# Key pass of a decoder step: value taps loaded later, a gate product moved, one-column factors in scalar form

## The reference

```python
def compress_rows(rows, w1, b1, w2):
    ...
    for j in range(CMP_PARTS):
        h = h + jnp.einsum('bnsgd,sdh->bngh', units[:, j:j + n_cmp], w1p[j])
    return jax.nn.gelu(h) @ w2
...
o_cmp, p_grp = cmp_branch(q, pos, kv['k_cmp'], kv['v_cmp'])
idx, ok = select_blocks(p_grp, pos, kv['n_slc'])
o_slc = kv['slc_fn'](q, pos, idx, ok)
o_win = kv['win_fn'](q, pos)
o = gates[:, :, 0] * o_cmp + gates[:, :, 1] * o_slc + gates[:, :, 2] * o_win
```

## Time and profile before

| what | value |
|---|---|
| median of 3 executions | 3237.72 us (3237.55 to 3238.18) |
| the profiled execution | 3232.46 us |
| its span, first to last instruction | 3230.3 us |
| mean granted clock of TensorE | 0.995 |
| PE busy | 3178.1 us, 98% |
| DVE busy | 1996.0 us, 62% |
| ACT busy | 1553.2 us, 48% |
| POOL busy | 519.0 us, 16% |
| mean DMA rate over the span | 188 GB/s |

### The profile page before, as it was taken

How to read it: one execution, slowest core, us unless ns; L and a number is a source line. 1 busy time by engine, 2 the same in 40 slices (tenths; PEclk the granted TensorE clock), 3 DMA queues, 4 the chain that set the end, 5 groups by cost and what they waited for, 6 DMA issues and landing times.

```text
span 3230.3 us, 69264 instructions
## 1 busy us (share of the span) xinstructions
PE 3178.1 (98%) x27708; PEld 3039.2 (94%) x27708; DVE 1996.0 (62%) x2283; ACT 1553.2 (48%) x1929; POOL 519.0 (16%) x476
## 2 busy tenths in 40 slices
PE   7999999999999999999999999999999999999998
PEld 6999899999999999999999997866999999999998
DVE  7888888865655544555675546465655554455566
ACT  4555555644544444444554533354554444444454
POOL 5666666500000000000000006000000000000000
PEclk9999999999999999999999999999999999999999
DMA  6445554466665556565556659898556555656553
GB/s 179 143 149 159 173 155 152 148 180 184 186 183 175 186 185 192 176 186 185 179 183 183 185 186 304 285 353 268 183 178 186 177 189 182 181 177 188 183 180 128
DMA packets 384393, 608.42 MB, mean 188 GB/s; under 512 B 52537, under 2 KB 144987, under 8 KB 383883
## 3 DMA queue, kind: packets, MB, share of 16 engines
q1 hardware_dynamic: 351738, 539.06, 53.2%
q10 hardware_dynamic: 29392, 60.86, 5.5%
q0 software_dynamic: 3024, 5.22, 0.5%
HBM read 594.83 MB, written 26.94 MB: 192 GB/s over the span
## 4 chain that ended last, share of the span: by engine, by line
PE 94%; DVE 2%; ACT 1%; DMA 1%; issue 1%; SPq 1%; POOL 0%; ACTq 0%; DVEq 0%; POOLq 0%
PE psum L429 23%; PE psum L431 23%; PE psum L430 23%; PE psum L1078 4%; PE psum L1080 3%; PE psum L1079 3%; PE psum L1057 3%; PE psum L2423 2%; PE psum L2433 1%; PE psum L2471 1%; PE psum L1135 1%; PE psum L2314 1%; PE psum L1161 1%; PE psum L2288 1%; PE psum L2302 0%
## 5 line engine op out<-in xcount | busy, mean ns | idle before, releaser
L396 DVE TENSOR_TENSOR w_rest<-w_raw,w_head 128x1024 fp32r<-128x1024 f32 x776 | 973.0, 1265 | 945.8 <-ACT w_head L392 945.0
L392 ACT ACTIVATE w_head<-w_raw 128x1024 fp32r<-128x1024 f32 x776 | 909.7, 1183 | 945.0 <-PE psum L431 931.6
L429 PE MATMUL psum<-act_head,w_head 128*128 128x264 f32 x4224 | 1205.1, 285 | 1.7 <-DVE act_rest L2881 1.7
L431 PE MATMUL psum<-act_head,w_rest 128*128 128x264 f32 x4224 | 1200.8, 284 | 0.0
L430 PE MATMUL psum<-act_rest,w_head 128*128 128x264 f32 x4224 | 1199.9, 284 | 0.0
L429 PEld LDWEIGHTS psum<-act_head,w_head 128*128 128x128 f32 x4224 | 821.9, 195 | 2.5 <-issue 2.1
L430 PEld LDWEIGHTS psum<-act_rest,w_head 128*128 128x128 f32 x4224 | 822.3, 195 | 0.1
L431 PEld LDWEIGHTS psum<-act_head,w_rest 128*128 128x128 f32 x4224 | 821.8, 195 | 0.0
L429 PE MATMUL psum<-hid_head,w_head 128*128 128x264 f32 x1408 | 400.6, 284 | 0.0
L431 PE MATMUL psum<-hid_head,w_rest 128*128 128x264 f32 x1408 | 399.9, 284 | 0.0
L430 PE MATMUL psum<-hid_rest,w_head 128*128 128x264 f32 x1408 | 399.5, 284 | 0.0
(11 more groups left out here) (433 smaller groups left out, 4006.8 us busy)
## 6 DMA issues: line engine op xcount, KB each, us to landing
w_raw<-in_ffn_w_gate SPq DMA_DIRECT2D x176, 512.0 KB, 4.4
w_raw<-in_ffn_w_up SPq DMA_DIRECT2D x176, 512.0 KB, 4.4
w_raw<-in_ffn_w_down SPq DMA_DIRECT2D x176, 512.0 KB, 3.7
w_raw<-in_cache_cmp_k SPq DMA_DIRECT2D x256, 128.0 KB, 2.6
w_raw<-in_cache_cmp_v SPq DMA_DIRECT2D x256, 128.0 KB, 2.6
w_raw<-in_ssm_w_glu SPq DMA_DIRECT2D x64, 512.0 KB, 4.5
w_raw<-in_ple_w_gate SPq DMA_DIRECT2D x64, 512.0 KB, 3.9
w_raw<-in_kv_w SPq DMA_DIRECT2D x48, 512.0 KB, 3.8
```

Source lines behind the costliest of these rows:

```text
L392: nc.scalar.activation(pairs(WH, u), tiles_of(RAW, u), ACT.Copy).then_inc(head_done, 1)
L396: nc.vector.tensor_tensor(pairs(WL, u), tiles_of(RAW, u), pairs(WH, u).bitcast(F32), ALU.subtract).then_inc(rest_done, 1)
L429: nc.tensor.matmul(o, wh, head, start=k == 0, stop=False)
L431: last = nc.tensor.matmul(o, wl, head, start=False, stop=k == UK * kunits - 1)
```

## The change

The change has three parts. The **value taps** are issued behind tiles 58 to 65, in place of 20 to 27, with a wait on SP for the key taps ahead of each; the key taps' products on PE then wait only for the first half of the taps, the value taps' products for all. The **gate product** of the compressed branch moves on DVE from unit 8 to unit 9, behind the copy of tile 9's keys. In **`factor_dve`** three of the four operations on one column have the form tensor with per-partition scalar in place of tensor with tensor, with the same numbers.

```diff
         if part == 0:
             pe.wait_ge(nt_used, SMALL_JOBS + len(ROW_JOBS))
-            pe.wait_ge(ld_taps, L_TAPS)
+            pe.wait_ge(ld_taps, L_TAPS // 2 if kv == 0 else L_TAPS)
             pe.wait_ge(ld_second, L_SECOND)
...
         f, new = DM[:, 7 + 4 * k:8 + 4 * k], DM[:, 24 + k:25 + k]
-        link_dve(dve, V.tensor_tensor(total, total, new, ALU.add))
+        link_dve(dve, V.tensor_scalar(total, total, new, None, ALU.add))
         link_dve(dve, V.reciprocal(f, total))
-        link_dve(dve, V.tensor_tensor(f, f, GSM[:, 1 + k:2 + k], ALU.mult))
-        link_dve(dve, V.tensor_tensor(new, new, f, ALU.mult))
+        link_dve(dve, V.tensor_scalar(f, f, GSM[:, 1 + k:2 + k], None, ALU.mult))
+        link_dve(dve, V.tensor_scalar(new, new, f, None, ALU.mult))
...
         if u == 8:
             dve.wait_ge(ld_rank, 16)
             link(V.tensor_tensor(RK[:, 0, :, :], RK[:, 0, :, :], EARL[:, :, :], ALU.mult))
+        if u == 9:
             dve.wait_ge(gates_moved, GATES_MOVED)
             sp_pe.wait(dve, "cmp turned")
             sp_dve.made_by(V.tensor_scalar(PCS[:, 1, 0:NCMP], PCS[:, 1, 0:NCMP], GSM[:, 0:1], None, ALU.mult), "cmp gated")
-        if u == 9:
             link(V.tensor_tensor(RK[:, 1, :, :], other, one, ALU.is_gt))
...
-            if 16 <= u < 24:
-                taps = slice(4 * (u - 16), 4 * (u - 16) + 4)
+            if 54 <= u < 62:
+                taps = slice(4 * (u - 54), 4 * (u - 54) + 4)
+                sp.wait_ge(ld_taps, L_TAPS // 2)
                 sp.dma_start(W1Q[:, taps, :], w1[1][taps].rearrange("t d h -> d t h")).then_inc(ld_taps, 16)
```

## The result

The change is **slower**: 3245.31 us median (12 executions, 3239.72 to 3254.85) against 3237.89 of the kernel before on the same chip (12 executions, 3233.01 to 3245.39). The profiled execution took 3246.33 us, span 3244.3.

What follows compares the result with a forecast made beforehand. PE was taken to bound the kernel, busy 98% of the span, so edits matter only at its waits. Terms 0 - 0.4 + 0.2 = -0.2 from the 3237.72 us median gave 3237.5, range 3233.6 to 3239.6.

Steps and rivals of the forecast that it cites:

- Edit one: Gate product from unit 8 to 9: PE's wait mostly returns a unit later and at tile 12; term 0.
- Edit two: Unit 24 factor chain: one-column scalar forms run free, L2736 still held by POOL, PE gains 0.38 us; term -0.4.
- one column still held: Rival: the scalar form waits for POOL even on one column in the factor chain; 3238.1 us, chance 0.15.
- DVE first: Rival: L2736 gets in ahead of POOL, PE's 2.28 us wait and the clock's 1.6 go; 3234.0 us, chance 0.12.
- Clock kept: Rival: the shorter 1.9 us wait in unit 25 brings no half rate, worth 1.6 us; 3235.9 us, chance 0.20.
- Edit three: Value taps behind tiles 58 to 65: last piece lands 2070.9, 0.6 us before PE asks; term +0.2, bounds 0 and +2.5.
- taps late: Rival: the last value tap lands after PE asks, PE stops once at unit 59's taps; 3239.3 us, chance 0.15.

Runs made afterwards that it cites:

- factor only: The kernel before with only the three one-column operations of the factor chain in scalar form: 3236.72 us against 3238.75, ratio 0.9999.
- taps behind 59: The kernel before with the value taps behind tiles 59 to 66: 3246.18 us against 3237.43, ratio 1.0027.
- taps only: The kernel before with only the value taps moved behind tiles 58 to 65, run twice: 3249.26 us (ratio 1.0039), then 3241.16 us (ratio 1.0013).
- the early kernel: The change with key taps behind tiles 20 to 27, value taps behind 28 to 35, factor chain in unit 25: 3231.29 us against 3237.43, ratio 0.9986.

## Why the prediction was wrong

The forecast was no measurable difference, with a range up to 3239.6; the median is 3245.31. By the order of its own steps:

- **Edit one.** The chain of waits came as forecast: the wait before the scores of unit 10 is 1.74, and that for tile 12 is 1.44 where 1.12 was worked out; its turning starts 23.81 us into the pass, 23.75 before, so the load did land when it had. The term of 0 left out the clock. I had priced half clock only for unit 25, though two waits so close together are 3.2 us of standstill. By the table it was half for 6.8 us here, 2.9 us of time. In the medians of the gate alone this is 1.3 us with an interval that holds 0, so its share of the loss isn't settled by them. The remark that the gates depend on POOL's transfers alone was incomplete: without the key taps beside them they come 1.06 us sooner in one profile and about as much in two others.
- **Edit two.** Right in mechanism and size: one-column forms free at 0.20 us, L2736 held and 0.29 us behind POOL, PE's wait shorter by 0.47 where 0.38 was forecast. The rivals "one column still held" and "DVE first" both fell. The page "VectorE: DVE Perf Modes" of the Trainium skill, section "What auto-detection actually checks", gives the two-port mode by the outermost non-unit dimension of source and destination. A one-column operand has no such dimension, so by the page's wording it isn't in that mode. The rows agree in that it doesn't wait for POOL: 0.20 and 0.21 us inside POOL's product in the change. "Clock kept" happened in two profiles with the shorter wait (factor only; the change with taps behind 54) and not in two others (the change; the same with taps behind 28); but it happened once with the wait of 2.26 as well (taps behind 59), so it isn't the edit's doing.
- **Edit three. This is the step that failed:** "less the 0.52 MB of tile 66 ... 7.78 MB must pass before the last piece has landed. At the 355 GB/s of a stretch with taps in it this takes 21.9 us: 2070.9." From that came a landing 0.6 us ahead of PE and a term of +0.2. In the run of this edit alone PE asks 6.67 us later in the span (2078.22 for 2071.55), and the same stretch, from about 2055.65 on, moved 8.32 MB at 345 GB/s in 24.1 us. The 8.30 MB before I took tile 66 off were right. Its 0.52 MB were asked for behind the last piece on the same queue, but 0.45 MB of them were through before the taps' last packet ended at 2079.11: the order holds for asking, not across the engines for landing. They are 1.5 us of the miss, and the rate is 0.7. So 0.6 us ahead became 1.54 late. In the change itself the wait is 1.77, in the second run of this edit 2.65, with the last piece behind tile 66 4.06. The term was +0.2, with bounds 0 and +2.5; the change shows 1.77 of wait and 1.5 for the half clock behind it, 3.2 in all, and for that clock the term had no price.
- **The rival "taps late"** named the right mechanism but priced it at 1.8 us in the end, as it had no price for the clock behind the wait. A wait of 1.5 to 2.7 us there brought 3.4 to 10.2 us at half clock, 1.5 to 4.4 us, and its chance of 0.15 was too low for what the text itself called a tie with nothing to cover it.
- **The sum** from the profile: gate place +0.2 and clock +2.9, unit 25 -0.5, taps +1.8 and clock +1.5, together 5.9 for the 5.5 that the key pass grew and the 7.4 of the medians. That the clock's share at the gate is as large in the median executions is argued, not shown. That the taps' place costs time is shown by three pairs of runs: about 5 us for taps only (both runs together) and for late taps on the early kernel, and 8 by the ratios for the change against itself with taps behind 28. With taps behind 54 the ratios differ by 3 us and their intervals overlap.

## What to carry to other kernels

A transfer moved towards its use gains nothing if its old place cost PE nothing. A landing time that is worked out from a mean rate to within 1 us of its use is too near: here four units more left 3.0 and 3.3 us in two profiles. Count what is asked for behind the transfer too, where the DMA engines are full. Each wait of PE by 1.5 us or more should be priced with the half clock that can follow it, which here cost about as much again or more, and so should two shorter waits close behind each other. Where work is held by a neighbour engine's operation, moving it to start later in that operation can all but free the engine that waits, though the work is still held (1.65 us, against 2.47 in the change and 0.49 unheld).

## What was unexpected of the hardware

- The length of the half clock doesn't go with the wait ahead of it: 1.47 us of idle was followed by 10.2 us, 1.54 and 1.77 by 3.4, 2.65 by 6.8, and with 4.06 came 13.7, all at the same place.
- A TENSOR_SCALAR on one column, its scalar from SBUF, ran in 0.20 to 0.21 us inside a POOL product, while the same kind of operation on 511 columns was held until 0.29 us after POOL's end, whether it started 0.17 or 1.01 us into it. A TENSOR_TENSOR on one column had been held for 2.27 us.
- Without key taps in the stretch, twelve small transfers of gates landed 1.06 us earlier, though the engines moved 355 GB/s at a share of 0.99 even then.
- Of a tile asked for behind the last taps on the same queue, 222 of 256 packets had ended before the taps' last one (taps only; 184 of 256 in the change).
